# Block 2's output projection in column halves, the context rows first into layer 1, and filling steps issued ahead of the scores

## What is computed

```python
# block 1, each layer
q, k, v, gates = split(rmsnorm(x) @ w_in)           # 24 heads of 64; 3 gates of 1024 columns
o_a, o_b, o_c = dilated(q, k, v), moba(q, k, v), stick_breaking(q, k, v)
x = x + (g0 * (o_a @ w_out_a) + g1 * (o_b @ w_out_b) + g2 * (o_c @ w_out_c)) @ w_o

# block 2, layer 0: for the 256 x tokens and the 256 context tokens
x = x + gate * (y @ w_out)                          # y: attention and hyena branch
x_ctx = x_ctx + c_gate * (y_ctx @ w_out)
# block 2, layer 1 (odd): context rows give keys and values only
h, h_ctx = modulated_norm(x), modulated_norm(x_ctx)
wq, wk, wv, nq, nk, nv, wg, ng = split(h @ w_in)
y = concat(windowed_gqa(wq, wk, wv) * silu(wg), neighbourhood(nq, nk, nv) * silu(ng))
x = x + gate * (y @ w_out)
```

## Time and profile before

| what | value |
|---|---|
| median of 3 runs | 1652.92 us (1646.65 to 1655.31) |
| the profiled execution | 1647.87 us |
| its span, first to last instruction | 1646.0 us |
| mean granted TensorE clock | 0.976 |
| TensorE busy | 1545.0 us, 94% |
| VectorE busy | 968.9 us, 59% |
| ScalarE busy | 784.5 us, 48% |

### The profile page before, as it was taken

One profiled execution on the slowest core, in us unless ns is written; L12 is line 12 of the kernel. 1 busy time (PEld: TensorE's weight loads), 2 busy tenths in 40 slices (PEclk: granted clock), 3 DMA queues, 4 the chain that ended last, 5 costly groups with the idle time before them and its releaser, 6 DMA issues.

```text
span 1646.0 us, 21049 instructions
## 1 busy us (share of the span) xinstructions
PE 1545.0 (94%) x8064; PEld 1225.7 (74%) x8064; DVE 968.9 (59%) x1736; ACT 784.5 (48%) x1327; POOL 64.4 (4%) x128
## 2 busy tenths in 40 slices
PE   6999998999999999989999998999978997899997
PEld 5887777899887878777899877677753476786675
DVE  4454457666445544458576555744777654974654
ACT  4546775455344446874465443444430013434552
POOL 4040000000000000000000000000000000400000
PEclk9999999999999999999999999999988999998999
DMA  8782335695556642335895554421120011541100
GB/s 257 241 177 93 116 109 185 209 270 188 195 188 225 210 155 101 109 96 188 260 243 191 194 166 125 120 74 55 52 64 13 0 35 43 161 128 52 52 1 26
DMA packets 182979, 220.92 MB, mean 134 GB/s; under 512 B 6476, under 2 KB 103286, under 8 KB 182817
## 3 DMA queue, kind: packets, MB, share of 16 engines
q1 hardware_dynamic: 179840, 211.65, 40.9%
q0 software_dynamic: 3040, 7.93, 2.4%
HBM read 216.54 MB, written 3.01 MB: 133 GB/s over the span
## 4 chain that ended last, share of the span: by engine, by line
PE 74%; DVE 14%; ACT 7%; issue 3%; DMA 2%; SPq 0%; DVEq 0%; ACTq 0%
PE bank L573 20%; PE bank L575 19%; PE bank L574 19%; PE bank L957 2%; DVE w_low L1606 2%; ACT w_high L1226 2%; PE bank L983 2%; PE bank L968 2%; PE bank L786 1%; PE bank L732 1%; DVE arena L1981 1%; PE bank L763 1%; PE bank L655 1%; DMA raw<-in_w_up 1%; PE bank L1088 1%
## 5 line engine op out<-in xcount | busy, mean ns | idle before, releaser
L1606 DVE TENSOR_TENSOR w_low<-raw,w_high 128x1024 fp32r<-128x1024 f32 x352 | 425.6, 1216 | 418.2 <-ACT w_high L1226 415.1
L1226 ACT ACTIVATE w_high<-raw 128x1024 fp32r<-128x1024 f32 x352 | 366.8, 1046 | 378.7 <-PE bank L575 314.5
L573 PE MATMUL bank<-w_high,acts_r 128*128 128x512 f32 (+1 forms) x896 | 357.3, 399 | 23.0 <-DVE acts_r L1623 6.0
L575 PE MATMUL bank<-w_high,acts_r 128*128 128x512 f32 (+1 forms) x896 | 347.7, 388 | 0.0
L574 PE MATMUL bank<-w_low,acts_r 128*128 128x512 f32 (+1 forms) x896 | 347.7, 388 | 0.0
L573 PE MATMUL bank<-acts_r,w_high 128*128 128x256 f32 (+1 forms) x736 | 231.6, 315 | 0.3 <-DVE w_low L1606 0.3
L575 PE MATMUL bank<-acts_r,w_low 128*128 128x256 f32 (+1 forms) x736 | 225.0, 306 | 0.0
L574 PE MATMUL bank<-acts_r,w_high 128*128 128x256 f32 (+1 forms) x736 | 224.9, 306 | 0.0
L573 PEld LDWEIGHTS bank<-w_high,acts_r 128*128 128x128 f32 x896 | 170.1, 190 | 66.1 <-DVE w_low L1606 13.1
L575 PEld LDWEIGHTS bank<-w_high,acts_r 128*128 128x128 f32 x896 | 169.2, 189 | 38.4
L574 PEld LDWEIGHTS bank<-w_low,acts_r 128*128 128x128 f32 x896 | 169.6, 189 | 33.5
(11 more groups left out here) (286 smaller groups left out, 1790.5 us busy)
## 6 DMA issues: line engine op xcount, KB each, us to landing
raw<-in_w_in SPq DMA_DIRECT2D x70, 1024.0 KB, 5.2
raw<-in_w_up SPq DMA_DIRECT2D x64, 512.0 KB, 6.8
raw<-in_w_down SPq DMA_DIRECT2D x32, 1024.0 KB, 5.0
raw<-in_w_ada SPq DMA_DIRECT2D x24, 1024.0 KB, 6.8
raw<-in_w_in SPq DMA_DIRECT2D x32, 512.0 KB, 5.2
raw<-in_w_o SPq DMA_DIRECT2D x8, 1024.0 KB, 7.7
raw<-in_w_out SPq DMA_DIRECT2D x8, 1024.0 KB, 5.1
raw<-in_w_out_c SPq DMA_DIRECT2D x4, 768.0 KB, 5.4
```

What stands on the lines that cost most here:

```text
L573: mm(o, lh, rh, start=start, stop=False)
L575: return mm(o, ll, rh, start=False, stop=stop)
L1226: run(A_(high, src, ACT.Copy), (high_ready, n + 1))
L1606: run(V.tensor_tensor(low, src, high.bitcast(F32), ALU.subtract), (split_ready, n + 1))
```

## The change

In block 1, eight filling steps are issued after the wait for the `qkv` copies and before the wait for the `qT` copies and the first scores.

In block 2, the output projection of layer 0 goes, for each column half, over the context tiles (2, 3) and then over the x tiles (0, 1); a half's four weight quarters stay in place for both. The context tiles are added to `X` and normed by themselves (norm 8, two tiles, four banks); their 16 transposes are issued within the last part, ahead of its k = 6. Their evacuation goes to a buffer of its own, `hT3c`; the x tiles follow as norm 6 into `hT3x`. VectorE adds the x tiles of the second column half after it has evacuated norm 8.

In layer 1 the slabs go 3, 4, 1, 0, 2, 5, 6 (loads too). Slab 3 is projected for the context tiles, then norm 6 is transposed, then for the x tiles. Heads are normalized in the order 3, 1, 0, 2, without `during`, and transposed: 3 after slab 1, 1 after slab 0, 0 after slab 2, then seven filling steps, then 2. The attention takes the remaining 57. GpSimd waits for bank 3 of the new norm 6 in place of bank 7 of the old.

```diff
-    slabs += [("in2", 1, c) for c in range(7)] + [("out2", 1, c) for c in range(2)]
+    slabs += [("in2", 1, c) for c in (3, 4, 1, 0, 2, 5, 6)] + [("out2", 1, c) for c in range(2)]
...
+        hT3x = carve([base], 2, KD, SEQ, of=acts_r, start=base)
+        hT3c = carve([20 * D], 2, KD, SEQ, of=hidden_r, start=qkv_at)
...
                 for c in range(6, 9):
                     for t in range(TILES):
                         pe.wait_ge(*emptied("qkv", l, c, t))
-                for j in range(2):
-                    for b in range(6):
-                        pe.wait_ge(*emptied("qT", l, j, b))
-
                 if l == 0:
                     pe.wait_ge(masks_loaded, MASKS * 16)
...
                 filler = gate_groups()
+                ended_in[(l, "at")] = []
+                advance(filler, 8)
+                for j in range(2):
+                    for b in range(6):
+                        pe.wait_ge(*emptied("qT", l, j, b))
                 for u in range(len(U) + 2):
...
-            def project_first(tiles):
-
-                acts = tiles_of(hT2)
+            def part_of_tiles(slab, name, acts, tiles, ready=None, during=None):
+
                 for k in range(KD):
-                    key = ("in2", 0, 0, k // 4, k // 2 % 2)
+                    key = slab + (k // 4, k // 2 % 2)
                     if k % 2 == 0:
                         wh, wl = (w.rearrange("p (k n) -> p k n", k=2) for w in split(*key))
...
+                    if during:
+                        during(k)
+                    if ready:
+                        pe.wait_ge(*ready(k))
                     for t in tiles:
-                        group = ("in2", 0, 0, t)
+                        group = (name,) + slab[1:] + (t,)
                         if k == 0:
                             open_bank(*group)
...
                     if k % 2 and tiles[0] == 0:
                         end_quarter(key, ins, *(group if k == KD - 1 else ()))
...
-            out2(0, range(T4), oT2r, yThr)
+            def turn_context(k):
+                if k == 6:
+                    norm_transposes(8, xn3[:, TILES:T4], TILES, 2)
+
+            outs = lambda k, t: tiles_of(oT2r)(k, t) if k < 4 else tiles_of(yThr)(k - 4, t)
+            for c in range(2):
+                part_of_tiles(("out2", 0, c), "out2", outs, (2, 3))
+                part_of_tiles(("out2", 0, c), "out2", outs, (0, 1), during=turn_context if c else None)
 
 
             gate_rows(1, 1)
-            norm_transposes(6, xn3, T4, 1)
+            part_of_tiles(("in2", 1, 3), "in2", layer_rows(1), (2, 3), ready=lambda k: emptied("hT", 8, k // 2))
+            norm_transposes(6, xn3, TILES, 2)
+            part_of_tiles(("in2", 1, 3), "in2", layer_rows(1), (0, 1), ready=lambda k: emptied("hT", 6, k // 2))
+            project2(1, 4, range(T4))
+            project2(1, 1, range(T4))
+            turn_heads(1, 3, lambda c, t: nk[:, t, c * P:(c + 1) * P], 4, T4, 1)
             project2(1, 0, range(TILES))
-            project2(1, 1, range(T4))
+            turn_heads(1, 1, lambda c, t: k3d[:, t, c, :], KVH, T4, 1)
             project2(1, 2, range(TILES))
-            project2(1, 3, range(T4))
             turn_heads(1, 0, lambda c, t: wq[:, t, c * P:(c + 1) * P], 4, TILES, 2)
...
+            filler = fill1()
+            advance(filler, 7)
             turn_heads(1, 2, lambda c, t: nq[:, t, c * P:(c + 1) * P], 4, TILES, 2)
...
-            attention2(1, fill1(), lambda u: 2)
+            attention2(1, filler, lambda u: 2)
...
-            splits.due("out2", 0, 1, T4 - 1)
+            splits.due("out2", 0, 1, 3)
+            act.wait_ge(*x_added.at("context"))
+            norm_guess(8, TILES, xn3[:, TILES:T4], x0=TILES)
+            norm_scale(8, TILES, xn3[:, TILES:T4], x0=TILES)
+            sequence_evacuate(8, 1, 1, hT3c)
+            splits.due("out2", 0, 1, 1, ahead=1)
             act.wait_ge(*x_added.at(5))
-            norm_guess(6, T4, xn3)
-            norm_scale(6, T4, xn3)
+            norm_guess(6, TILES, xn3)
             gate_rows(1, gate_b1, 1)
-            modulated_evacuate(6, 1)
...
+            norm_scale(6, TILES, xn3)
+            sequence_evacuate(6, 1, 0, hT3x)
...
-            add_gated(0, 5, list(range(T4)), gate_b0)
-            run.settle()
-
-            norm_finish(6, T4, xn3)
-            modulated_evacuate(6, 1, mod_tmp3)
-            heads_norm(1, 0, wq, TILES, QH, 2, True, None, [("in2", 1, 0, t) for t in range(TILES)], ("in2", 1, 1, T4 - 1))
-            heads_norm(1, 1, kv3[:, :, 0:KVH * DH], T4, KVH, 3, True, k3d, [("in2", 1, 1, t) for t in range(T4)], ("in2", 1, 2, TILES - 1))
-            heads_norm(1, 2, nq, TILES, QH, 4, False, None, [("in2", 1, 2, t) for t in range(TILES)], ("in2", 1, 3, T4 - 1))
-            heads_norm(1, 3, nk, T4, QH, 5, False, None, [("in2", 1, 3, t) for t in range(T4)])
+            dve.wait_ge(*emptied("gateB", 0, 1, 1))
+            add_gated(0, 5, (0,), (2, 3, 0, 1), gate_b0)
+            add_gated(0, "context", (1,), (2, 3), gate_b0)
+            norm_finish(8, TILES, xn3[:, TILES:T4], x0=TILES)
+            sequence_evacuate(8, 1, 1, hT3c, mod_tmp3)
+            add_gated(0, 5, (1,), (0, 1), gate_b0)
+            splits.due("out2", 0, 1, 1, ahead=1)
+            norm_finish(6, TILES, xn3)
+            sequence_evacuate(6, 1, 0, hT3x, mod_tmp3)
+            heads_norm(1, 3, nk, T4, QH, 5, False, None, [("in2", 1, 3, t) for t in (2, 3, 0, 1)])
+            heads_norm(1, 1, kv3[:, :, 0:KVH * DH], T4, KVH, 3, True, k3d, [("in2", 1, 1, t) for t in range(T4)])
+            heads_norm(1, 0, wq, TILES, QH, 2, True, None, [("in2", 1, 0, t) for t in range(TILES)])
+            heads_norm(1, 2, nq, TILES, QH, 4, False, None, [("in2", 1, 2, t) for t in range(TILES)])
...
-            pool.wait_ge(*filled("hT", 6, 7))
+            pool.wait_ge(*filled("hT", 6, 3))
```

More of the change, by code:

```diff
@@ L2046, in attention2, with add_gated @@
                     take_features(l, key)
-            def add_gated(l, n, tiles, gate_b):
-                for c in range(2):
+            def add_gated(l, n, columns, tiles, gate_b):
+                for c in columns:
                     for t in tiles:
```

127 lines of the change are left out of this document (52 added, 75 removed).

## The result

| what | before | after |
|---|---|---|
| median | 1652.74 us (4 runs, 1646.65 to 1655.31) | 1672.17 us (4 runs, 1667.74 to 1675.96) |
| ratio | | 1.0121, 95% interval 1.0100 to 1.0143 |
| span of the profiled execution | 1646.0 us | 1665.8 us |
| mean granted TensorE clock | 0.976 | 0.968 |

What follows compares the result with a forecast made beforehand. TensorE, busy 94% of the span, was taken as the bound. Block 1's steps +5.0, clock +2.0 and block 2's second layer -2.6 summed to +4.4 us, so 1657 us; range 1650 to 1662, eight in ten 1646 to 1666.

Steps and rivals of the forecast that it cites:

- The front of block 1: Ahead of block 1's scores: the 2.88 us wait stays, gain 0, and eight steps add 5.6 us per layer.
- The clock term: Block 1's two empty C units: lower TensorE clock costs +2 us for both layers, bounds 0 and some 9.
- (b): Block 1's attention tail: without the gate work it takes 7.7 us instead of 9.77, returning 2.1 us per layer.
- Rival 1: Clock falls in block 1's empty units, +9 to 11 us for both layers, total 1664 to 1666; chance 0.22.
- part 2: Block 2's second layer: +0.3 until the attention and -2.9 behind its start, in all -2.6 us, bounds -10 to +5.
- Term (a): Last C ring of block 1: 1.04 us per layer comes back, as no weight quarter comes free there.
- Part 2 until the attention: Block 2's second layer: 9.8+5.4+2.8 us of waits become 5.1+1.2+2.4+8.2+1.3; attention starts at 1497.6, against 1497.3 before.
- the bank wait: Slab 3's first products in block 2 wait for banks VectorE empties late: 5.1 us idle, plus 2.3 for the clock.
- The seven steps' 2.9 us: End of block 2's second attention: fewer steps in the last units save 2.4 us, last split and silu 0.5.
- Part 1's sum: Eight steps ahead of block 1's scores: +5.6-1.0-2.1 = +2.5 us per layer, +5.0 for two, clock +2 besides.
- The signs: Right: named waits and gaps in both blocks. Wrong: front wait gone, ring under 4.5 us, attention over 5 us off.

Runs made afterwards that it cites:

- useless products: The changed kernel plus twelve products nobody reads in each of the last two C units of both block 1 layers; 1667.23 us, ratio 1.0081.
- block 1 only: The kernel before plus only the change's eight steps ahead of block 1's scores; 1664.97 us, ratio 1.0067.
- the run with the three splits put off: Block 2's change with another bank order, without block 1's edit, three weight-quarter splits moved behind slab 2's head norms; 1655.45 us, ratio 1.0009 to before.
- the run with steps from the A units: The changed kernel, its eight early steps per block 1 layer taken from the A units instead of the C units; 1657.32 us, ratio 1.0024.
- block 1 undone: The changed kernel without the eight steps ahead of block 1's scores; 1658.75 us, ratio 1.0029 to before.
- the steps spread: The run with the context copies early, its seven early steps taken from seven units spread over block 2's second attention; 1647.62 us, ratio 0.9945.
- the last run: The run with the context copies early, without the seven filling steps ahead of the last head transposes; 1645.39 us, ratio 0.9930.
- the context copies early: The run with the three splits put off, with ScalarE copying slab 3's two context tiles before norm 6's evacuation; 1650.96 us, ratio 0.9979.
- one addition left: The run with the steps spread, with only one of GpSimd's sixteen mask additions kept; 1646.60 us, ratio 0.9945.

## Why the prediction was wrong, point by point

**The front of block 1** was right. The 2.88 us stay as 2.82 and 2.71, because the wait left in place ends last, and the steps come on top: +5.60 us in layer 1. In layer 0 it is +7.05, as the clock fell behind the wait: 3.5 us at 0.51 in the window, and eight steps in 7.13 us, where layer 1 has them in 5.77.

**The clock term is the step that failed.** I had +2 us for both layers, and with it a return (b) of 2.1 us a layer for the gates' work that no longer stands in the tail. The return was right at full clock: I chained 7.7 us, and layer 1 with the useless products measured 7.58. In the change it was 11.44. Half clock on the chain's TensorE pieces makes up the difference of 3.7 us: the second part (2.07 us to the end of L754, before 1.15), the last values (1.5, before 0.9), L814 (3.65, before 1.94) and L658 (2.49, before 1.92). A return of 2.1 turned into a loss of 1.7 us in layer 0, and of 0.6 in layer 1, where the tail had been partly at half clock already. With 0.9 us in the last ring of layer 1 and 1.4 behind the front wait of layer 0, the clock took 8.8 us from my sum, where I had 2.

Rival 1 named this mechanism, with a chance of 0.22, and its price was right: 9 to 11 us of clock on top of +5.0, so 14 to 16 for block 1, and the two profiles show 15.7 (the ratios 11 to 15). Its total of 1664 to 1666 fell short by part 2, 4.8 us where the sum had -2.6. What was wrong is the chance, which rested on one of two layers having held its clock behind rings as idle. Those rings had four filling steps each, the empty ones have none: the windows of before were no bound for them. Behind empty units all six tails on record (the change, block 1 only, the change without the seven steps) took 11.04 to 11.44 us. Behind filled ones, in the kernel before and nine runs, the transposes were at half clock too, in 19 of 20 tails (3.2 to 3.7 us); yet 18 of those tails took 9.76 to 9.90 us, because the gates' work sets their end: even at full clock TensorE waits there 1.48 us for VectorE. The layer that I took as proof of a held clock was the exception, and what the empty units changed is that the low clock starts earlier and has no such wait to hide in. The sentence on "TensorE: Matmul & The Clock Gate" of the Trainium skill (activity releases the slow default) pointed this way and should have had the greater weight; the trace agrees with it here, 0.55 and 0.56 in the two tails.

**Term (a)**, 1.04 us less in the last ring, came to 1.00 in layer 0 only (4.68 against 5.68). Half clock on the second part gave it back in layer 1 and in the four rings of the two other versions with empty units, 5.61 or 5.62 us each. My reason, the missing rounding L1249, does not explain all either: with useless products there is no L1249, and the ring is 5.63, as the filling itself stands in it. And what I did not price: ScalarE's copies of the gates' banks fall into other units than before. Four of them stand in the first C unit now, its second part comes 1.0 us later and the next 1.4, and the 0.9 left of it ahead of the last ring gave back what (a) brought.

**Part 2 until the attention** was nearly right. The 9.8 us wait went, the bank wait came (4.83 for the first product, forecast 4.4), then 1.68 (1.2), 2.25 (2.4), 6.23 (8.2) and 1.19 (1.3) us; the start of the attention is 1.2 us late where I had 0.3. VectorE's queue sets it: the run with the three splits put off moved it by 4.3 us, for a forecast of 3.7.

**Behind the attention's start** part 2 failed in two terms. The seven steps' 2.9 us did not return: the attention lasts 114.9 us from the first scores to L1019 (before: 114.65 to L1009), since the low clock lasts 20.5 us instead of 10.3, and the empty last units show gaps of 1.18 and 1.03 us at L978. Then 96 products of the last projection take 2.8 us more, at 0.88. In the forecast of part 2 the clock stood behind one wait only; here it fell ahead of the first units and behind the empty last ones too. In the change without the seven steps the last projection keeps 1.00, but the low clock at the attention's start lasts 27 us, and the time is the same.

**Part 1's sum** should have read, for layers 0 and 1: front +5.6 each, clock behind it +1.4 and 0, rings -0.1 and +0.9, tail +1.7 and +0.6, in all 8.7 and 7.0 us, where I had 2.5 a layer and 2 for the clock of both.

**The signs** that I had named for a right forecast came in nearly all: the front wait at 128, gaps of 3.31 and 2.57 us in the last two C units of layer 0, 4.83 us on VectorE ahead of slab 3, no 9.8 us wait, 6.23 us ahead of the last transposes. None of the signs of being wrong did. They looked at waits, and what went wrong was the pace between them.

## What to carry to other kernels

Work moved ahead is free only if it is taken from where the same engine is the bound. Eight steps ahead of the scores cost nothing that the ratios show when full units lent them, and 11 to 15 us when they came out of rings that they had filled: there their time does not come back, and the clock falls over what follows. When a rotation of banks decides a wait, count to the bank's last user: a swap only moves the wait to the next opener until every copy in the chain is early enough. And for a queue that sets a start, first take from it what is not needed yet: another bank order, three splits put off, two copies put forward and no steps ahead together turned 1.0029 into 0.9930.

## What the runs showed that I had not expected

- A wait of the same length is followed by half clock in one place and not in another. In the change, 2.82 us at 128 us: 3.5 us at 0.51; 2.71 us at 620 us: none. In the run with steps from the A units, 2.92 us at the same place of layer 0: none there. The kernel before had none behind its two waits of 2.88 us, block 1 undone behind both, with 1.5 and 2.7 us lost. So the clock behind one wait is not a fixed price. How the low clock at the second attention's start gets its length (10.3 us before, 20.5 after, 23.9 with the steps spread and 27.4 in the last run) stays open. The wait ahead of it does not tell: with the context copies early it was 4.13 us and the low clock 10.2 us long, with the steps spread 3.05 and 23.9 us.
- GpSimd slows VectorE's small steps more than its large ones. A 128x32 `tensor_scalar` took 0.65 us beside it and 0.18 with one addition left, a 128x512 multiply of two SBUF inputs 1.22 and 0.69, and the 128x2048 reduction 2.29 in both. "SBUF — State Buffer" of the Trainium skill, in the section on who interferes with whom, says that a reduction does not contend while two-input operations and `tensor_scalar` in its faster mode do, each blocked for the other's whole instruction. The trace agrees for the reduction and the multiply; in which mode this `tensor_scalar` ran it does not show, only that it was held up as well. Small and large step lose about the same, 0.47 and 0.53 us, beside additions of 0.9 us each, so the price does not go by the length of VectorE's own instruction.
- The kernel before ranged from 1647.74 to 1661.08 us over 31 runs, and its profiled execution was 5 us under the median of its own set. Without many runs of both on one chip, none of the differences of 0.3% could be read, and the two least ones could not be told apart even so.
